# Routed experts on one core: tokens kept as a high and a low part, and one gather of 256 columns for every two rounds

## The chip, the core and the metric

The kernel runs on one core of a Trainium2 chip. A core has five engines with their own instruction streams: TensorE (PE: matmuls, with PEld its weight loads), VectorE (DVE), ScalarE (ACT), GpSimd (POOL, all but unused here) and SyncE (SP), which issues the DMA transfers from the chip's memory. They meet at semaphores. TensorE writes its results to eight PSUM banks of 128 x 512 floats, which ACT and DVE empty. The metric is the device time of one execution in microseconds (us).

## The reference

The reference is a whole two-block network over 256 tokens of width 1024. The part that matters is the last layer's mixture of experts. A router gives each token two of eight experts; expert e applies its own gated feed-forward net, and the token's result is the sum of its two experts' outputs, weighted by the router:

```python
h = rmsnorm(x, g)                      # 256 x 1024
top, idx = top_k(h @ router, 2); w = softmax(top)
for e in range(8):
    rows = tokens that chose e         # at most 128 in a round
    y[rows] += w * ((silu(h[rows] @ w_gate[e]) * (h[rows] @ w_up[e])) @ w_down[e])
x = x + gate * y                       # then a last rmsnorm
```

(The lines are a paraphrase. `w_gate` and `w_up` are 1024 x 3072, `w_down` 3072 x 1024, all float32.)

## The kernel before

All the rest of the network comes first and is not touched. `routed_feed_forward` computes the layer in **rounds**. A round takes one expert and up to 128 of its tokens. There is one round for each expert (0 to 7), and up to three more for experts with over 128 tokens; with these inputs there are 8 rounds. Round 0 is written out; rounds 1 to 7 are one loop on every engine, whose count is read from a table that the router's results fill.

**Weights.** A round reads 36 **tiles** of 1 MB: `n` = 0 to 23 are gate and up weights (for each of six `j`: two gate tiles, two up tiles), 24 to 35 are down weights. SP loads a tile into one of four `wide` buffers as soon as DVE has finished with the tile that lay there. Precision is kept by splitting each float32 operand into two parts of the type float32r, on which TensorE works faster: ACT copies the tile to `wide_high` (rounded, L3739), DVE subtracts that from the tile to get `wide_low` (L3864), each in one of three buffers, and TensorE does 12 matmuls of 512 columns a tile: high x high (L3588), high x low (L3589), low x high (L3592). ACT may fill a `wide_high` buffer when TensorE has used the tile three before.

**Tokens.** `h_tokens` (`ht`) holds all 256 tokens of the layer, in float32. At the start of a round the round's tokens are needed in the first 128 columns of an operand, `xg_high` and `xg_low` (`x_hi`, `x_lo`). A *gather* picks them: a matmul of `ht` with a matrix of zeros and ones, `pick` (256 tokens x 128 places), in float32: 16 matmuls of 128 columns, into banks 6 and 7. Then ACT copies the banks to `x_hi` (L3714) and DVE subtracts to get `x_lo` (L3816). The gather of round k + 1 stands in round k's down part, after its sixth tile (`q == 5`, so tile 29), and its copies stand behind tile 32 on ACT and DVE. The last round gathers too, for a round that does not come. DVE makes the `pick` of the next round at tile 8 (L3779), and TensorE transposes `pick` for the way back after tile 3 (`turn_pick`).

**Results.** After a round's last tile ACT scales and rounds the output to `y_high` (L3724), DVE makes `y_low` (L3810), and TensorE *scatters* them back to the 256 tokens: 16 matmuls of 256 float32r columns (L3619, L3620), into banks 1, 3, 6 and 7. This is done in the next round, after its tiles 0 and 1. DVE adds the banks to `x` (L3822). The banks 0 and 1 (gate) and 2 and 3 (up) are used in turn by the j's, 4 and 5 hold the output, and 6 and 7 the transposed hidden values (L3632).

What each engine does is an order written out by hand; no scheduler changes it. Within a round DVE does, for each `n`, `low_tile(n)` first, and behind it at n = 1 the two `y_low`, at n = 3 to 6 two additions to `x` each, and at n = 8 `pick`; ACT does at n = 1 the two `y_high`.

## Time and profile before

| | |
|---|---|
| time, median of 3 runs | 2598.43 us (2598.34 to 2603.25) |
| the profiled execution's own time | 2601.54 us |
| its span, first to last instruction | 2599.7 us |
| stretch of the expert rounds | 1721 to 2586 us |
| period of a round | 107.0 us |
| PE busy in the span | 2542.3 us (98%) |
| DVE, ACT busy | 1987.1 us (76%), 1428.3 us (55%) |
| moved by DMA | 627.19 MB, 241 GB/s over the span |

A round's period is the distance between the starts of the gathers in the chain that ended last. The profile is one execution, whose own time lies 3.1 us above the median of the three. Busy time of the PE rows counts a matmul from its start to its modelled end, and matmuls overlap; how fast they follow each other is read from their starts.

### The profile page before, as it was taken

How to read it: one execution, taken by the hardware profiler on the slowest of the kernel's cores; microseconds unless marked ns; L12 is line 12 of the kernel's file. 1: busy time of each engine (PE TensorE's matmuls, PEld its weight loads, DVE VectorE, ACT ScalarE, POOL GpSimd, SP SyncE). 2: the span in 40 equal slices, each digit the busy share in tenths (PEclk: the TensorE clock that was granted, in tenths of full speed). 3: DMA queues.
4: the chain of work that ended last, by engine and by line, in shares of the span. 5: the costliest groups of instructions: out<-in, count | busy, mean ns of one | idle time of the engine just before them, and what ended most of it. 6: DMA issues, size and time to landing. Idle time of an engine off the chain costs nothing. (4 is left out here: it accounts for less than half of the span.)

```text
span 2599.7 us, 41703 instructions
## 1 busy us (share of the span) xinstructions
PE 2542.3 (98%) x14574; PEld 2213.4 (85%) x14574; DVE 1987.1 (76%) x2776; ACT 1428.3 (55%) x1835; POOL 0.2 (0%) x4
## 2 busy tenths in 40 slices
PE   9999999998999999999999999999999999999998
PEld 5798889897888888888889999878888888888887
DVE  6688378896787777776856645569889889898897
ACT  4654243384544444444544434457777677777775
POOL 0000000000000000000000000000000000000000
PEclk8999899999999999999999999999999999999999
DMA  8423335425788878776434555359999999999995
GB/s 344 150 98 105 117 126 159 140 81 175 241 294 295 300 266 289 266 282 211 145 127 135 185 180 166 108 202 371 337 354 358 343 373 339 353 361 338 353 359 223
DMA packets 223747, 627.19 MB, mean 241 GB/s; under 512 B 15344, under 2 KB 23568, under 8 KB 223376
## 3 DMA queue, kind: packets, MB, share of 16 engines
q1 hardware_dynamic: 223632, 625.64, 68.6%
q8 instruction: 75, 1.23, 0.2%
q14 instruction: 40, 0.33, 0.0%
HBM read 619.29 MB, written 6.29 MB: 241 GB/s over the span
## 5 line engine op out<-in xcount | busy, mean ns | idle before, releaser
L3864 DVE TENSOR_TENSOR wide_low<-wide,wide_high 128x2048 fp32r<-128x2048 f32 x288 | 657.8, 2290 | 98.5 <-ACT wide_high L3739 96.4
L3739 ACT ACTIVATE wide_high<-wide 128x2048 fp32r<-128x2048 f32 x288 | 552.4, 1918 | 198.8 <-PE bank L3592 131.5
L232 DVE TENSOR_TENSOR expert_tile_low<-slot,expert_tile_high 128x1024 fp32r<-128x1024 f32 x216 | 263.6, 1223 | 119.2 <-ACT expert_tile_high L224 115.6
L224 ACT ACTIVATE expert_tile_high<-slot 128x1024 fp32r<-128x1024 f32 x216 | 227.4, 1054 | 182.1 <-PE bank L242 64.1
L3588 PE MATMUL bank<-wide_high,xg_high 128*128 128x512 f32 x768 | 303.8, 396 | 2.5 <-DVE xg_low L3816 2.5
L3589 PE MATMUL bank<-wide_high,xg_low 128*128 128x512 f32 x768 | 300.2, 391 | 0.0
L3592 PE MATMUL bank<-wide_low,xg_high 128*128 128x512 f32 x768 | 205.7, 390 | 0.0
L241 PE MATMUL bank<-h_high,expert_tile_high 128*128 128x256 f32 x704 | 173.4, 284 | 0.0
L2102 PE MATMUL bank<-expert_tile_high,act_hi 128*128 128x512 f32 x512 | 161.6, 397 | 11.9 <-DVE act_lo L2253 11.9
L242 PE MATMUL bank<-h_low,expert_tile_high 128*128 128x256 f32 x704 | 172.6, 283 | 0.0
L3588 PEld LDWEIGHTS bank<-wide_high,xg_high 128*128 128x128 f32 x768 | 144.8, 189 | 31.4 <-DVE xg_low L3816 2.7
L3592 PEld LDWEIGHTS bank<-wide_low,xg_high 128*128 128x128 f32 x768 | 144.1, 188 | 30.5 <-DVE wide_low L3864 0.2
L3589 PEld LDWEIGHTS bank<-wide_high,xg_low 128*128 128x128 f32 x768 | 144.9, 189 | 29.0
L2102 PE MATMUL bank<-expert_tile_high,act_lo 128*128 128x512 f32 x512 | 160.0, 394 | 0.0
L3588 PE MATMUL bank<-wide_high,moe_hid_high 128*128 128x512 f32 x384 | 151.7, 395 | 0.0
L3589 PE MATMUL bank<-wide_high,moe_hid_low 128*128 128x512 f32 x384 | 149.7, 390 | 0.0
L241 PEld LDWEIGHTS bank<-h_high,expert_tile_high 128*128 128x128 f32 x704 | 134.3, 191 | 13.0 <-issue 10.1
L232 DVE TENSOR_TENSOR layer_tile_low<-slot,layer_tile_high 128x1024 fp32r<-128x1024 f32 x66 | 80.9, 1226 | 80.0 <-ACT layer_tile_high L224 80.0
L2184 ACT ACTIVATE act_hi<-act_g 128x256 fp32r<-128x256 f32 x128 | 52.9, 413 | 159.4 <-DVE act_g L2248 158.8
L2108 PE MATMUL bank<-expert_tile_low,act_hi 128*128 128x512 f32 x512 | 138.2, 392 | 0.0
L242 PEld LDWEIGHTS bank<-h_low,expert_tile_high 128*128 128x128 f32 x704 | 134.7, 191 | 2.9
L224 ACT ACTIVATE layer_tile_high<-slot 128x1024 fp32r<-128x1024 f32 x66 | 70.1, 1062 | 112.5 <-PE bank L242 106.6
(611 smaller groups left out, 5129.8 us busy)
## 6 DMA issues: line engine op xcount, KB each, us to landing
wide<-in_moe_gu SPq DMA_DIRECT2D x192, 1024.0 KB, 6.0
wide<-in_moe_d SPq DMA_DIRECT2D x96, 1024.0 KB, 6.3
slot<-in_peer_u SPq DMA_DIRECT2D x128, 512.0 KB, 4.5
slot<-in_peer_v SPq DMA_DIRECT2D x128, 512.0 KB, 4.6
slot<-in_w_in SPq DMA_DIRECT2D x72, 512.0 KB, 3.6
picked_or_ada<-in_ada_w SPq DMA_DIRECT2D x48, 512.0 KB, 5.1
ada_slot<-in_ada_w SPq DMA_DIRECT2D x48, 512.0 KB, 4.7
slot<-in_ffn_gu SPq DMA_DIRECT2D x48, 512.0 KB, 3.6
```

The costliest lines, as they stand in the source:

```text
L224: core.nc.scalar.activation(self.tile_hi[:, place % 2], core.slot[u][:], ACT.Copy).then_inc(self.hi_ready.sem, 1)
L232: core.nc.vector.tensor_tensor(self.tile_lo[:, place % 2], slot[:], self.tile_hi[:, place % 2].bitcast(F32), ALU.subtract)\
L241: nc.tensor.matmul(out(c), self.tile_hi[:, place % 2, c, :], high(c), start=opens(c), stop=False, skip_group_check=not whole)
L242: last = nc.tensor.matmul(out(c), self.tile_hi[:, place % 2, c, :], low(c), start=False, stop=False, skip_group_check=not whole)
L2102: last = nc.tensor.matmul(core.bank[4 + 2 * tt + b][:, :], tokens(part, tt), v_hi[:, b, :], start=False, stop=False, skip_group_check=True)
L2108: last = nc.tensor.matmul(core.bank[4 + 2 * tt + b][:, :], tokens(act_hi, tt), v_lo[:, b, :], start=False, stop=stop, skip_group_check=True)
L2184: nc.scalar.activation(act_hi[:, w, :], act_g[:, w, :], ACT.Copy).then_inc(act_high.sem, 1)
L3588: nc.tensor.matmul(out(s), high(s), part(hi, s), start=s in opens, stop=False, skip_group_check=True)
L3589: nc.tensor.matmul(out(s), low(s), part(hi, s), start=False, stop=False, skip_group_check=True)
L3592: last = nc.tensor.matmul(out(s), high(s), part(lo, s), start=False, stop=s in closes, skip_group_check=True)
L3739: nc.scalar.activation(w_hi[n % NB][:].rearrange("p c n -> p (c n)"), wide[n % U][:], ACT.Copy).then_inc(hi_ready.sem, 1)
L3864: nc.vector.tensor_tensor(w_lo[n % NB][:].rearrange("p c n -> p (c n)"), wide[n % U][:], w_hi[n % NB][:].rearrange("p c n -> p (c n)").bit ...
```

## The change

The change touches `routed_feed_forward` alone.

- **Tokens as two parts.** `ht` is split once, in round 0: ACT copies it to `ht_hi` (behind its tile 8), DVE subtracts to get `ht_lo` (behind its tile 9), which takes the room of `ht`. From then on a gather is float32r: `ht_hi` with `pick` gives the high part in one bank, `ht_lo` with `pick` the low part in another. ACT and DVE each copy their own bank, and DVE no longer waits for ACT.
- **Rounds in pairs.** The rounds are now FIRST (0), then a loop of three over a pair EVEN and ODD (1 and 2, 3 and 4, 5 and 6; the names count within a pair), then a loop ALONE over the rest (7 and any more). `pick`, `x_hi` and `x_lo` hold two rounds side by side. DVE makes two `pick`s at n = 8 of FIRST and ODD, one in ALONE, none in EVEN.
- **Where the gathers are.** No round gathers at tile 29 any more. EVEN opens with `gather_two` (32 matmuls of 256 columns, in four groups of eight), and the scatter of the round before stands right behind it, before tile 0. ODD gathers nothing, and scatters after its tiles 0 and 1, as before. ALONE opens with `gather_alone` (32 matmuls of 128 columns), then the scatter. FIRST keeps the float32 gather.

```diff
+            def gather_two(i):
+                pe.wait_ge(picks.sem, picks.at(2) + i)
+                pe.wait_ge(hid_ready.sem, hid_ready.at(J) + i * (2 * J))
+                for g in range(4):
+                    if g == 3:
+                        pe.wait_ge(x_high.sem, x_high.at(1) + opened(EVEN, i))
+                        pe.wait_ge(x_ready.sem, x_ready.at(1) + opened(EVEN, i))
+                    for part, bank in ((ht_hi, GATHERED[g][0]), (ht_lo, GATHERED[g][1])):
+                        for j in range(2):
+                            c = 2 * g + j
+                            for tt in range(2):
+                                last = nc.tensor.matmul(core.bank[bank][:, 2 * M * j:2 * M * j + 2 * M], part[:, tt, c * P:c * P + P],
+                                                        pick[:, tt].rearrange("p r m -> p (r m)"), start=(tt == 0), stop=(tt == 1))
+                    last.then_inc(gathered.sem, 1)
+    GATHERED = ((6, 7), (1, 3), (0, 2), (6, 7))
+    GATHERED_ALONE = ((0, 6), (2, 7))
...
+            def scatter(k, kind, i):
                 pe.wait_ge(backs.sem, backs.at(1) + k)
-                pe.wait_ge(x_ready.sem, x_ready.at(2) + k * 2)
                 for s in range(4):
                     if s % 2 == 0:
                         pe.wait_ge(y_split.sem, y_split.at(s // 2 + 1) + k * 2)
+                    if kind == EVEN:
+                        pe.wait_ge(x_high.sem, x_high.at((2, 2, 4, 4)[s]) + opened(kind, i))
+                        pe.wait_ge(x_ready.sem, x_ready.at((2, 2, 4, 4)[s]) + opened(kind, i))
+                    if kind == ALONE and s >= 2:
+                        pe.wait_ge(x_ready.sem, x_ready.at(s - 1) + opened(kind, k))
...
+                if kind == EVEN:
+                    gather_two(i)
+                if kind == ALONE:
+                    gather_alone(k)
+                if kind in (EVEN, ALONE):
+                    scatter(k, kind, i)
...
-                    if q == 5:
-                        pe.wait_ge(hid_ready.sem, hid_ready.at(J) + k * J)
-                        gather(k + 1)
...
+            def copy_two(i):
+                for g in range(4):
+                    act.wait_ge(gathered.sem, gathered.at(g + 1) + opened(EVEN, i))
+                    nc.scalar.activation(x_hi[:, 2 * g:2 * g + 2, :, :], core.bank[GATHERED[g][0]][:, :].rearrange("p (c r m) -> p c r m", c=2, r=2), ACT.Copy)\
                         .then_inc(x_high.sem, 1)
...
+                    if n == C and kind == FIRST:
+                        nc.scalar.activation(ht_hi[:], ht[:], ACT.Copy).then_inc(tokens_high.sem, 1)
...
+            def low_two(i):
+                for g in range(4):
+                    dve.wait_ge(gathered.sem, gathered.at(g + 1) + opened(EVEN, i))
+                    nc.vector.tensor_copy(x_lo[:, 2 * g:2 * g + 2, :, :], core.bank[GATHERED[g][1]][:, :].rearrange("p (c r m) -> p c r m", c=2, r=2))\
+                        .then_inc(x_ready.sem, 1)
...
+                    if n == C + 1 and kind == FIRST:
+                        dve.wait_ge(tokens_high.sem, tokens_high.at(1))
+                        nc.vector.tensor_tensor(ht_lo[:], ht[:], ht_hi[:].bitcast(F32), ALU.subtract).then_inc(tokens_low.sem, 1)
```

`copy_two` stands behind `keep_outputs` (the two `y_high`) at ACT's n = 1, and `low_two` behind the two `y_low` at DVE's n = 1; before, both copies stood at n = 32.

On TensorE, in the down part of a round of the kernel before (L3588, L3589 and L3592 are a tile's three kinds of matmul, L3605 the gather), the program has:

```order
L3588 MATMUL bank<-wide_high,moe_hid_high 128x512
L3589 MATMUL bank<-wide_high,moe_hid_low 128x512
L3592 MATMUL bank<-wide_low,moe_hid_high 128x512 x4
L3605 MATMUL bank<-pick,h_tokens 128x128 x16
L3588 MATMUL bank<-wide_high,moe_hid_high 128x512
L3589 MATMUL bank<-wide_high,moe_hid_low 128x512
```

On TensorE, in the changed kernel, between the last tile of the round before and tile 0 of an EVEN round (L3640 is the new gather, L3671 and L3672 the scatter, L3611 a tile's last four matmuls), it has:

```order
L3611 MATMUL bank<-wide_low,moe_hid_high 128x512 x4
...
L3640 MATMUL bank<-pick,h_tokens_high 128x256 x4
L3640 MATMUL bank<-pick,h_tokens_low 128x256 x4
L3640 MATMUL bank<-pick,h_tokens_high 128x256 x4
L3640 MATMUL bank<-pick,h_tokens_low 128x256 x4
L3640 MATMUL bank<-pick,h_tokens_high 128x256 x4
L3640 MATMUL bank<-pick,h_tokens_low 128x256 x4
L3634 ISA
L3640 MATMUL bank<-pick,h_tokens_high 128x256 x4
L3640 MATMUL bank<-pick,h_tokens_low 128x256 x4
...
L3671 MATMUL bank<-back,y_high 128x256
```

The gather has left the middle of the down part and stands at the seam of two rounds, where its last group (behind the wait of L3634) uses banks 6 and 7 a second time.

On DVE, at tile 1 of an EVEN round of the changed kernel (L3955 is `wide_low`, L3889 `y_low`, L3907 the copies of the low parts), the program has:

```order
L3955 TENSOR_TENSOR wide_low<-wide,wide_high 128x2048
L3888 ISA
L3889 SCALAR_TENSOR_TENSOR y_low<-bank,shares_of_places,y_high 128x512
L3888 REGISTER_ALU
L3889 SCALAR_TENSOR_TENSOR y_low<-bank,shares_of_places,y_high 128x512
L3906 ISA
L3907 CAST xg_low<-bank 128x512
...
L3955 TENSOR_TENSOR wide_low<-wide,wide_high 128x2048
```

Four such copies now stand between `y_low` and the `wide_low` of tile 2, which before followed `y_low` at once.

On DVE, in round 0 of the changed kernel, from tile 8 on (L3858 is `pick`, L3964 the split of the tokens, L3986 the hidden values), the program has:

```order
L3858 TENSOR_SCALAR pick<-const,first,place_cols 128x128 x4
L3885 COPY shares_of_tokens<-shares 128x2
L3955 TENSOR_TENSOR wide_low<-wide,wide_high 128x2048
L3964 TENSOR_TENSOR h_tokens_low<-h_tokens,h_tokens_high 128x2048
L3986 TENSOR_TENSOR hid_r<-silu_r,bank 128x512
L3955 TENSOR_TENSOR wide_low<-wide,wide_high 128x2048
```

Two more `pick`s and the split of `ht` stand between the low parts of tiles 8 and 10.

## Rows read from the trace of the kernel before

**Rows 1.** The page, part 1: busy time and share of the span.

```profile
span 2599.7 us, 41703 instructions
PE 2542.3 (98%) x14574; PEld 2213.4 (85%) x14574; DVE 1987.1 (76%) x2776; ACT 1428.3 (55%) x1835; POOL 0.2 (0%) x4
```

**Rows 2.** Windows: one round, part of it, and a stretch around a gather.

```profile
core 0: us, PE busy (x) PEld busy (x) DVE busy (x) ACT busy (x) POOL busy (x), PEclk, DMA share, GB/s
1942.00:2049.00 107.00, 107.00 (x512) 89.51 (x510) 94.88 (x66) 77.23 (x53) 0.00 (x0) 1.00 0.98 353
1957.00:2020.00 63.00, 63.00 (x291) 52.11 (x290) 58.07 (x41) 46.35 (x32) 0.00 (x0) 1.00 0.99 353
1814.00:1819.00 5.00, 5.00 (x40) 4.72 (x39) 4.15 (x3) 3.07 (x4) 0.00 (x0) 1.00 1.01 392
```

**Rows 3.** Waits in the rounds (1721 to 2600): us in total, times, longest.

```profile
ACT wide_high L3739 <- PE bank L3592: 131.5, 151, 2.3
ACT wide_high L3739 <- DMA wide<-in_moe_gu: 37.2, 48, 3.1
ACT wide_high L3739 <- DMA wide<-in_moe_d: 29.2, 28, 1.8
PE bank L3588 <- DVE xg_low L3816: 2.5, 1, 2.5
PEld bank L3592 <- DVE wide_low L3864: 0.2, 1, 0.2
```

**Rows 4.** Chain that ended last, in order of time: start, us, what.

```profile
1815.11 3.57 PE bank L3605 x32
...
1922.23 3.57 PE bank L3605 x32
...
2564.43 3.57 PE bank L3605 x32
```

**Rows 5.** Timeline of PE around a scatter, 1840 to 1843: start, us, engine.

```profile
1840.29 0.28 PE L3619 MATMUL bank<-back,y_high 128*128 128x256 f32 x1
...
1842.08 0.28 PE L3620 MATMUL bank<-back,y_low 128*128 128x256 f32 x1
...
1842.20 0.40 PE L3588 MATMUL bank<-wide_high,xg_high 128*128 128x512 f32 x1
```

**Rows 6.** Groups by line and form, 1700 to 2600: busy, mean ns, idle before.

```profile
L3605 PE MATMUL bank<-pick,h_tokens 128*128 128x128 f32 x288 | 33.7, 275 | 0.8 <-DVE pick L3779 0.8
L3816 DVE TENSOR_TENSOR xg_low<-bank,xg_high 128x512 fp32r<-128x512 f32 x18 | 11.5, 682 | 0.0
L3714 ACT ACTIVATE xg_high<-bank 128x512 fp32r<-128x512 f32 x18 | 10.4, 589 | 6.9 <-PE bank L3605 6.8
L3880 DVE CAST back<-bank 128x256 fp32r<-128x256 f32 x8 | 3.3, 414 | 0.0
```

**Rows 7.** Timelines of PE, ACT and DVE where round 2 begins.

```profile
1941.06 1.07 PE L3592 MATMUL bank<-wide_low,moe_hid_high 128*128 128x512 f32 x4
1941.97 0.39 PE L3588 MATMUL bank<-wide_high,xg_high 128*128 128x512 f32 x1
1941.72 1.27 ACT L3724 ACTIVATE y_high<-bank,shares_of_places 128x512 fp32r<-128x512 f32 x2 [0.35 <-PE bank L3592]
1943.68 1.40 DVE L3810 SCALAR_TENSOR_TENSOR y_low<-bank,shares_of_places,y_high 128x512 fp32r<-128x512 f32 x2
1945.00 4.48 DVE L3864 TENSOR_TENSOR wide_low<-wide,wide_high 128x2048 fp32r<-128x2048 f32 x2
```

**Rows 8.** Timelines of round 0: ACT tiles 8, 9; DVE tiles 9, 10; PE tile 10.

```profile
1747.46 1.91 ACT L3739 ACTIVATE wide_high<-wide 128x2048 fp32r<-128x2048 f32 x1
1752.09 0.60 DVE L3779 TENSOR_SCALAR pick<-const,first,place_cols 128x128 f32<-128x128 f32 x2
1752.66 2.29 DVE L3864 TENSOR_TENSOR wide_low<-wide,wide_high 128x2048 fp32r<-128x2048 f32 x1
1754.87 0.68 DVE L3887 TENSOR_TENSOR hid_r<-silu_r,bank 128x512 f32<-128x512 f32 x1
1755.46 2.29 DVE L3864 TENSOR_TENSOR wide_low<-wide,wide_high 128x2048 fp32r<-128x2048 f32 x1
1759.94 1.07 PE L3592 MATMUL bank<-wide_low,xg_high 128*128 128x512 f32 x4
```

**Rows 9.** Timeline of DVE and PE where the weights came latest.

```profile
1890.05 2.29 DVE L3864 TENSOR_TENSOR wide_low<-wide,wide_high 128x2048 fp32r<-128x2048 f32 x1 [2.39 <-ACT wide_high L3739]
1892.43 0.93 PE L3592 MATMUL bank<-wide_low,xg_high 128*128 128x512 f32 x3
```

More of the change, by code:

```diff
@@ L3537, in routed_feed_forward, with opened @@
         "outputs_low", "outputs_scattered", "outputs_added", "share_columns", "picks_turned"))
+    tokens_high, tokens_low = core.count("tokens_high"), core.count("tokens_low")
+    PAIRED = (EXPERTS - 2) // 2
+    FIRST, EVEN, ODD, ALONE = range(4)
+    ALONE_FROM = 2 * PAIRED + 1
+    def opened(kind, i):
+        return 0 if kind == FIRST else i * 4 + 2 if kind == EVEN else i * 2 + (2 + 4 * PAIRED - 2 * ALONE_FROM)
+    place_of = lambda kind: 1 if kind == ODD else 0
     J = D_FF // 512
@@ L3566, in _ @@
             sp.wait_ge(table_made.sem, table_made.at(1))
-            with sp.Fori(1, n_rounds(sp)) as k:
+            with sp.Fori(0, PAIRED) as i:
+                for r in range(1, 3):
+                    load(i * 2 + r, i * 2 + r, 0)
+            with sp.Fori(ALONE_FROM, n_rounds(sp)) as k:
                 load(k, expert_of(sp, k), 0)
@@ L3686, in round_ @@
                     else:
-                        turn_pick(k)
+                        turn_pick(k, place)
                 for q in range(T2):
@@ L3694, in round_ @@
                         turn(k, J - 1)
-                    if q == 5:
-                        pe.wait_ge(hid_ready.sem, hid_ready.at(J) + k * J)
-                        gather(k + 1)
             pe.sem_inc(scattered.sem, 4)
-            round_(0)
+            round_(0, FIRST, 0)
             pe.wait_ge(table_made.sem, table_made.at(1))
-            with pe.Fori(1, n_rounds(pe)) as k:
-                round_(k)
-            scatter(n_rounds(pe))
+            with pe.Fori(0, PAIRED) as i:
+                round_(i * 2 + 1, EVEN, i)
+                round_(i * 2 + 2, ODD, i)
+            with pe.Fori(ALONE_FROM, n_rounds(pe)) as k:
+                round_(k, ALONE, None)
+            scatter(n_rounds(pe), FIRST, None)
             for c in range(C):
@@ L3753, in round_ @@
                             .then_inc(hid_high.sem, 1)
-                    if n == 1 and not isinstance(k, int):
+                    if n == 1 and kind != FIRST:
                         keep_outputs(k)
-                    if n == 32:
-                        copy_gathered(k + 1)
+                        if kind == EVEN:
+                            copy_two(i)
+                        if kind == ALONE:
+                            copy_gathered(kind, k)
             act.sem_inc(y_kept.sem, 2)
             high_tile(0, 0)
-            copy_gathered(0)
-            round_(0)
+            copy_gathered(FIRST, 0)
+            round_(0, FIRST, 0)
             act.wait_ge(table_made.sem, table_made.at(1))
-            with act.Fori(1, n_rounds(act)) as k:
-                round_(k)
+            with act.Fori(0, PAIRED) as i:
+                round_(i * 2 + 1, EVEN, i)
+                round_(i * 2 + 2, ODD, i)
+            with act.Fori(ALONE_FROM, n_rounds(act)) as k:
+                round_(k, ALONE, None)
             keep_outputs(n_rounds(act))
@@ L3774, in _, with make_picks @@
         def _(dve):
-            def make_pick(k):
-                e = k if isinstance(k, int) else expert_of(dve, k)
-                for tt in range(2):
-                    ins = nc.vector.tensor_scalar(pick[:, tt, :], core.iota, first[:, bass.ds(k, 1)], place_cols[:, tt, bass.ds(e, 1)],
-                                                  ALU.add, ALU.is_equal)
+            def make_picks(k, n=1):
+                for r in range(n):
+                    e = k + r if isinstance(k, int) else expert_of(dve, k + r)
+                    for tt in range(2):
+                        ins = nc.vector.tensor_scalar(pick[:, tt, r, :], core.iota, first[:, bass.ds(k + r, 1)], place_cols[:, tt, bass.ds(e, 1)],
+                                                      ALU.add, ALU.is_equal)
                 ins.then_inc(picks.sem, 1)
@@ L3900, in _ @@
             take_shares(0)
-            low_gathered(0)
-            round_(0)
-            with dve.Fori(1, n_rounds(dve)) as k:
-                round_(k)
+            low_gathered_first()
+            round_(0, FIRST, 0)
+            with dve.Fori(0, PAIRED) as i:
+                round_(i * 2 + 1, EVEN, i)
+                round_(i * 2 + 2, ODD, i)
+            with dve.Fori(ALONE_FROM, n_rounds(dve)) as k:
+                round_(k, ALONE, None)
             rounds = n_rounds(dve)
```

104 lines of the change are left out of this document (67 added, 37 removed).

## Prediction

> **What bounds the kernel now.** I read the page first: TensorE is busy 98% of the span [rows 1]. Then the windows of one round: TensorE 107.00 of 107.00 us at a granted clock of 1.00, which is the level of 2.4 GHz, DVE 94.88, ACT 77.23, and the DMA share 0.98 [rows 2]. The table of waits says who waits: ACT waits 131.5 us for TensorE to use tiles, TensorE 2.5 us once for the first `xg_low`, and 0.2 us for a tile [rows 3]. So the rounds last as long as TensorE's instructions do, and an instruction taken from it is time won, unless DVE or the DMA, both near their limit, then come too late.
>
> **What is removed.** The chain shows each gather inside a round as one piece of 3.57 us [rows 4]; there are eight, of rounds 0 to 7, and the last serves no round. That is 8 x 3.57 = 28.6 us. The copies behind them (two of 589 ns on ACT, two of 682 ns on DVE [rows 6]) were hidden behind matmuls and give nothing by themselves.
>
> **What an EVEN round's opening costs.** The new gather has 32 float32r matmuls of 256 columns, each with its own weights. The scatter has the same form: 16 matmuls between 1840.29 and 1842.20 [rows 5], so 0.119 us each. A group of eight is 0.96 us, all of it 3.82 us. But the operands are needed at once. Let 0 be the seam, 1941.97 in the row of L3588. ACT has finished `y_high` at 1942.99, at 1.0. DVE is in `wide_low` of tile 1, then `y_low`, and is free at 1945.00, at 3.0 [rows 7]. From there:
> TensorE does groups 0 to 2 from 0 to 2.9, and must then wait: group 3 takes banks 6 and 7 again, so ACT and DVE must both have emptied them. ACT did so at about 1.8. DVE begins at 3.0; a copy of 512 columns costs 0.68, since 256 take 414 ns and the old subtraction of 512 took 682 [rows 6]. So group 3 runs from 3.75 to 4.7, after a wait of about 0.9. The first two parts of the scatter use banks 1 and 3, empty by then: 4.7 to 5.65. The last two need DVE's fourth copy, which begins when group 3 has drained, at 4.9, and ends at 5.6: no wait. They end at 6.6, and tile 0 starts. Of this the scatter's 1.9 us was paid before too, two tiles later. An opening adds 4.7 us, three add 14.1. The bounds: 3.8 each if DVE is early (11.5 in all), 6.5 each if every group waits for its copies (19.5).
>
> Queued behind the copies on DVE is `wide_low` of tile 2, and behind that SP's load of tile 6. ACT is free at 5.6, so it has split tile 2 at 7.5, and DVE at 9.8. TensorE does four matmuls in 0.91 us, 1941.06 to 1941.97 [rows 7], so a tile in 2.73, and comes to the low part of tile 2 at 6.6 + 2 x 2.73 + 1.8 = 13.9. That stall is hidden by 4 us. DVE has less in hand at tiles 6 to 11, where the additions to `x` and the hidden values stand between the tiles; I count it about 1 us ahead at tile 7, and cost it at nothing. If that cover went, it would be about 1 us a pair.
>
> **What the ALONE round's opening costs.** Its 32 matmuls have 128 columns, and no row shows float32r that narrow; each such matmul in the program has 256 or 512 columns. The lower end is the float32 gather's rate per instruction: x288 are 9 gathers of 32, and 3.57 / 32 is 0.112 us [rows 4, 6], which gives 3.6 us. The upper end is its rate per matmul (two instructions each), 0.223 us: 7.1 us. I take 7.0, from the only rows with the same 128 columns, the same weights and the same `pick`. The waits for `y_low` and the copies fall within it, and the scatter behind it is only moved. A rule of the Trainium skill speaks for the lower end: TensorE: Matmul & The Clock Gate, section "LDWEIGHTS", puts a load of 128 columns of weights at P / 1.2, 107 ns, and knows no surcharge for narrow float32r. By it the gather would take 3.4 us; no row here decides it.
>
> **What round 0 pays.** ACT splits `ht` behind tile 8: the form is a tile's, 1.91 us from about 1749.4 [rows 8], and tile 9 is high at 1753.1 and not 1751.7. DVE does four `pick`s where it did two (+0.5), `wide_low` of tile 9 until 1755.5, `ht_lo` as long as a tile's subtraction (2.2 net) to 1757.7, the hidden value to 1758.3, and then tile 10, ready at 1760.6. TensorE wants it at 1759.94 [rows 8]: it waits 0.6 us, and about nothing at tile 11. Bounds 0 and 3. Later ODD rounds make four `pick`s too, but have no split.
>
> **What the DMA costs.** The gather's pause let the weights catch up. Without it a round is 103.5 us, and 36 tiles must land every 2.87 us instead of 2.97, in the down part every 2.73. The windows show 353 GB/s at a share of 0.98 in a round, but 392 GB/s around a gather [rows 2], which is a tile in 2.68 us, so the engines can do more than they are asked. At the worst place `wide_low` was ready at 1892.34 and TensorE took it at 1892.43 [rows 9]. Such a dip now has no gather to heal it; I add 0.5 us, bounds 0 and 8. The Trainium skill speaks against the change here: HBM Reference, section "Specifications (TRN2)", gives a core 358 GB/s as its share. At that rate 36 tiles take 105.4 us, so each of the four rounds that no opening lengthens would lose 1.9 us, 7.7 in all. The window of 392 GB/s says that this is no cap for us; the page itself says that a core streaming alone gets about 425.
>
> **The sum.** -28.6 + 14.1 + 7.0 + 0.6 + 0.5 = -6.4 us. The profiled execution took 2601.5, so it would take 2595.1. It lay 3.1 above the median of 2598.4; the same difference from the median gives 2592.0 us, or 0.25% less. What measurement of this kernel can tell from no change is about 0.2%, 5.2 us: 2593.2.
>
> **Rivals.**
> *Narrow matmuls run at full pace.* ALONE's gather then costs 3.8 (32 x 0.119), and the time is 2588.8. For it: 256 columns take 0.119 us and 512 take 0.228 (0.91 / 4), so the time goes by the width [rows 5, 7]. Against it: no row is that narrow.
> *The openings or the loads cost more.* The copies run in step with the groups (+5.4 us at the upper bound), or a few tiles come late after a seam without a pause (+1 to +6). For it: the DVE is the busiest engine next to TensorE, and ACT already waits 37.2 + 29.2 us for tiles [rows 3]. Against it: TensorE waited for a tile 0.2 us in 860. The time is 2594 to 2598, about 2596.
> *Slower: the transfers take over.* If 353 GB/s is what they can give (a share of 0.98 to 0.99 [rows 2] reads so), 36 tiles take 107 us whatever TensorE does. Then the 28.6 us are not won, but for the last gather's 3.6; and as SP may load only when DVE has split, which the copies delay, a part of the openings is added. With half of them, (14.1 + 7.0) / 2 + 0.6 - 3.6 = +7.6: 2606. It decides once tiles land slower than one in 2.87 us over a whole round. Against it are the 392 GB/s, and that ACT waits twice as long for TensorE as for tiles [rows 3].
>
> **How the numbers follow.** As computed, within 1.5 us: 0.50. Narrow at full pace: 0.20. Openings or loads dearer: 0.20. Slower: 0.08. Something that wins more than all of this: 0.02. The likeliest is 2592.0 us. The first case is faster by over 0.2% in about three quarters (0.38), the second is, the last is: 0.60. Same: 0.12 of the first, and 0.19 of the third: 0.31. Slower: 0.09. The range of 2588.0 to 2597.5 takes in the first two, nearly all of the third, and leaves out some 0.12.
>
> **What would show it.** The gather's matmuls of 256 columns follow each other at 0.12 us, with one idle time of about 0.9 us in each of three openings, ended by DVE's copy of the low part; 6.6 us from the seam to tile 0. ALONE's gather takes 7 us (a pace of 0.22) or under 4 (0.12). One wait of about 0.6 us for `wide_low` of tile 10 in round 0. The pair of rounds has a period of about 212 us (2 x 103.5 + 4.7) where it was 214. The prediction is wrong if 256 columns of `pick` are slower than 256 of `back`, if TensorE waits for tiles in the rounds' down parts, or if the narrow gather costs other than its bounds.

## The result and the profile after

The changed kernel is slower: 2612.08 us, the median of 5 runs (2606.08 to 2622.31), against 2598.43 us (2596.04 to 2603.25, 5 runs) for the kernel before beside it. The ratio is 1.0060 with a 95% interval of 1.0044 to 1.0075. The forecast was 2592.0 us, faster. The profiled execution, at 2606.08 us, is the fastest of the five; a second trace of this kernel comes with the experiments.

The page, busy time and share, answers to [rows 1]:

```profile
span 2604.3 us, 41430 instructions
PE 2536.0 (97%) x14446; PEld 2204.8 (85%) x14446; DVE 1988.0 (76%) x2777; ACT 1428.6 (55%) x1834; POOL 0.2 (0%) x4
```

TensorE is busy 6.3 us less than before, and yet the span is 4.6 us longer: idle time came. The windows (us, busy of each engine, granted clock, DMA share, GB/s) of one stretch as long as in [rows 2], and of the openings of rounds 1, 3 and 5, show where:

```profile
1942.00:2049.00 107.00, 103.95 (x481) 86.56 (x480) 92.84 (x64) 74.95 (x51) 0.00 (x0) 0.98 0.96 350
1822.00:1840.00 18.00, 14.67 (x81) 13.23 (x80) 12.96 (x10) 8.85 (x9) 0.00 (x0) 0.91 0.84 286
2041.00:2057.00 16.00, 12.67 (x66) 11.28 (x65) 9.84 (x9) 9.16 (x9) 0.00 (x0) 0.79 0.86 315
2259.00:2278.00 19.00, 13.37 (x66) 12.07 (x65) 10.19 (x9) 9.18 (x9) 0.00 (x0) 0.73 0.69 255
```

In the three stretches around these openings TensorE is idle 3.3 to 5.6 us each, and the granted clock, 1.00 in every window of [rows 2], is 0.91, 0.79 and 0.73. The table of waits over the rounds (us in total, times, longest), beside [rows 3]:

```profile
ACT wide_high L3810 <- DMA wide<-in_moe_gu: 79.4, 88, 4.1
ACT wide_high L3810 <- PE bank L3611: 71.4, 85, 3.2
ACT wide_high L3810 <- DMA wide<-in_moe_d: 52.2, 59, 2.7
PE bank L3640 <- issue: 9.0, 4, 4.5
PE bank L3640 <- DVE xg_low L3907: 3.3, 1, 3.3
PE bank L3671 <- DVE y_low L3889: 1.4, 2, 1.1
PE bank L3607 <- ACT xg_high L3779: 1.0, 1, 1.0
PE bank L3611 <- DVE wide_low L3955: 0.6, 2, 0.4
```

Three readings. ACT waits twice as long for tiles as before (131.6 against 66.4 us), but TensorE waits for a tile only 0.6 us: the transfers became tight and did not take over. TensorE waits once for the low copies, for 3.3 us, where three waits of 0.9 were forecast. And it waits 9.0 us for "issue", that is for nothing which the profile records; there is no such wait inside the rounds before. The name alone proves little: at the first tile of round 0 a wait of 2.5 us is put down to `xg_low` in the trace of before, and one of 2.6 us to "issue" in seven of the other traces, three of them without a loop of pairs.

To compare kernels whose first 1,720 us differ a little from run to run, I split the expert stage of each trace. A tile is marked by the start of its last four matmuls (low x high); two tiles without anything between them are 2.72 us apart. The **opening** of a round is the distance from tile 35 to tile 0 less 2.72; a round's **inside** runs from tile 0 to tile 35. For round 3 of the changed kernel the timeline gives both marks, and an opening of 2056.84 - 2041.85 - 2.72 = 12.27 us:

```profile
2041.85 1.07 PE L3611 MATMUL bank<-wide_low,moe_hid_high 128*128 128x512 f32 x4
2056.84 1.07 PE L3611 MATMUL bank<-wide_low,xg_high 128*128 128x512 f32 x4
```

| kernel (profiled run) | openings of rounds 1 to 7 | openings, sum | insides, sum | stage |
|---|---|---|---|---|
| before | 0 in all | 0 | 832.7 | 851.7 |
| changed | 10.8, 0, 12.3, 0.1, 15.3, 0, 6.4 | 44.9 | 797.8 | 861.8 |

(The stage runs from tile 0 of round 0 to tile 35 of round 7: openings, insides and seven times 2.72 us.) The insides gave back 34.9 us. That is the eight gathers (28.6) and four scatters that moved into openings (4 x 1.96 = 7.8), less 1.5 us of new waits. The openings took 44.9 us for it, of which 7.8 are the moved scatters. The stage is 10.1 us longer and the span only 4.6, since round 0's first tile came 5.6 us earlier in this execution.

**How an opening is lost.** Timelines of TensorE, ACT and DVE at the opening of round 1, which no jump back precedes (start, us, engine, line):

```profile
1827.02 0.64 PE L3640 MATMUL bank<-pick,h_tokens_high 128*128 128x256 f32 x4
1829.38 0.64 PE L3640 MATMUL bank<-pick,h_tokens_low 128*128 128x256 f32 x4
1833.35 0.96 PE L3640 MATMUL bank<-pick,h_tokens_high 128*128 128x256 f32 x4 [3.33 <-DVE xg_low L3907]
1834.11 1.05 PE L3640 MATMUL bank<-pick,h_tokens_low 128*128 128x256 f32 x4
1826.97 1.92 ACT L3810 ACTIVATE wide_high<-wide 128x2048 fp32r<-128x2048 f32 x1 [1.74 <-DMA wide<-in_moe_gu]
1828.79 1.25 ACT L3795 ACTIVATE y_high<-bank,shares_of_places 128x512 fp32r<-128x512 f32 x2
1828.99 2.29 DVE L3955 TENSOR_TENSOR wide_low<-wide,wide_high 128x2048 fp32r<-128x2048 f32 x1 [1.37 <-ACT wide_high L3810]
1831.20 1.40 DVE L3889 SCALAR_TENSOR_TENSOR y_low<-bank,shares_of_places,y_high 128x512 fp32r<-128x512 f32 x2
1832.52 1.88 DVE L3907 CAST xg_low<-bank 128x512 fp32r<-128x512 f32 x3
```

Read it from the bottom. DVE's first copy of gathered tokens starts at 1832.52, because `y_low` and, ahead of it, the split of tile 1 come first in its order. DVE began to split tile 1 at 1828.99, because ACT had waited 1.74 us for that tile to land. The seam was at 1827.02, so `y_low` starts 4.2 us behind it; at the seam of [rows 7] it was 1.7. TensorE has done three groups by 1830.0 and stands still for 3.33 us. What follows is slow as well: four matmuls take 0.85 us (1834.96 - 1834.11) where the same four took 0.47 before the pause.

At the opening of round 3 a jump back of the loop comes first. Timelines of TensorE and DVE:

```profile
2045.96 1.22 PE L3640 MATMUL bank<-pick,h_tokens_high 128*128 128x256 f32 x4 [3.05 <-issue]
2046.98 1.05 PE L3640 MATMUL bank<-pick,h_tokens_low 128*128 128x256 f32 x4
2050.66 0.58 PE L3640 MATMUL bank<-pick,h_tokens_high 128*128 128x256 f32 x1 [0.28 <-issue]
2052.94 0.28 PE L3671 MATMUL bank<-back,y_high 128*128 128x256 f32 x1
2047.03 2.29 DVE L3955 TENSOR_TENSOR wide_low<-wide,wide_high 128x2048 fp32r<-128x2048 f32 x1 [1.46 <-ACT wide_high L3810]
2049.24 1.40 DVE L3889 SCALAR_TENSOR_TENSOR y_low<-bank,shares_of_places,y_high 128x512 fp32r<-128x512 f32 x2
```

TensorE does nothing for 3.05 us, waiting for no other engine by the profile, and then works at half pace. No wait for `xg_low` is left at this opening: DVE's copies are done before TensorE comes to them. Windows of short stretches show its granted clock, ahead of the pause in round 1 and behind the pauses of rounds 1, 3 and 5:

```profile
1826.00:1827.00 1.00, 1.00 (x6) 0.82 (x5) 1.00 (x1) 0.03 (x1) 0.00 (x0) 1.00 1.02 389
1833.00:1836.00 3.00, 2.65 (x13) 2.68 (x14) 2.09 (x4) 0.80 (x2) 0.00 (x0) 0.60 0.99 316
2046.00:2051.00 5.00, 4.72 (x20) 4.42 (x21) 3.97 (x4) 3.27 (x5) 0.00 (x0) 0.50 1.07 383
2265.00:2274.00 9.00, 7.71 (x34) 7.42 (x35) 4.88 (x7) 2.14 (x5) 0.00 (x0) 0.50 0.75 276
```

0.50 is the level of 1.2 GHz. The queues of the DMA engines have the other half of the story: packets that carry instructions. First before, from 1715 to 1942 (round 0 and the first pass of its loop); from 1942 to 2585 the view of that kernel shows no instruction packet at all:

```profile
q8 instruction: 9, 0.15, 0.2%
q14 instruction: 7, 0.06, 0.1%
```

And the changed kernel, from 1942 to 2585:

```profile
q8 instruction: 29, 0.48, 0.3%
q14 instruction: 16, 0.13, 0.0%
```

(Packets, MB, share.) A loop body of one round is fetched once; one of two rounds is fetched again in every pass: of the 29 packets on q8, 10 move between 2042 and 2258 us and 11 between 2260 and 2480, which are the second and the third pass. One of them moves right behind each jump back, from 2043.3 to 2044.3 us (TensorE starts again at 2045.96) and from 2262.4 to 2263.5 (it starts at 2265.19).

### The profile page after: what moved, and what is told of

Its sections match the earlier page's. It is cut to its first block and busy times, and to the rows that moved or that the text cites. A ratio compares the mean times of both kernels' runs of the same rounds, so it can differ in the third digit from the quotient of the medians.

```text
span 2604.3 us, 41430 instructions
## 1 busy us (share of the span) xinstructions
PE 2536.0 (97%) x14446; PEld 2204.8 (85%) x14446; DVE 1988.0 (76%) x2777; ACT 1428.6 (55%) x1834; POOL 0.2 (0%) x4
## 5 line engine op out<-in xcount | busy, mean ns | idle before, releaser
L3955 DVE TENSOR_TENSOR wide_low<-wide,wide_high 128x2048 fp32r<-128x2048 f32 x288 | 656.6, 2288 | 102.1 <-ACT wide_high L3810 97.2
L3611 PE MATMUL bank<-wide_low,xg_high 128*128 128x512 f32 x768 | 206.2, 390 | 0.6 <-DVE wide_low L3955 0.6
L3611 PEld LDWEIGHTS bank<-wide_low,xg_high 128*128 128x128 f32 x768 | 143.5, 188 | 32.5 <-DVE wide_low L3955 2.5
L241 PEld LDWEIGHTS bank<-h_high,expert_tile_high 128*128 128x128 f32 x704 | 134.9, 192 | 13.1 <-issue 10.1
```

The source lines that it names most:

```text
L241: nc.tensor.matmul(out(c), self.tile_hi[:, place % 2, c, :], high(c), start=opens(c), stop=False, skip_group_check=not whole)
L3611: last = nc.tensor.matmul(out(s), high(s), part(lo, s), start=False, stop=s in closes, skip_group_check=True)
L3955: nc.vector.tensor_tensor(w_lo[n % NB][:].rearrange("p c n -> p (c n)"), wide[n % U][:], w_hi[n % NB][:].rearrange("p c n -> p (c n)").bit ...
```

## The experiments

The theory after this reading had three parts: **A**, TensorE stalls at a jump back of a long body, since its instructions have to be fetched again; **D**, the copies stand behind a tile 1 that lands late (the first four expectations call it B, seams); and the half clock, which follows from either pause. The rivals: the transfers of the weights (**C**), and the gather's own cost. (Some later expectations give B and C another meaning and say which.) Each run's table row gives the median, the ratio to the kernel before in the same job with its 95% interval, and the split of its trace.

| run | median us | ratio | openings of 1, 3, 5, 7 | others | insides | stage |
|---|---|---|---|---|---|---|
| two-round bodies | 2600.36 | 1.0007 (0.9998 to 1.0016) | 0, 1.1, 1.2, 0 | 0 | 832.7 | 854.0 |
| changed, written out | 2604.09 | 1.0023 (1.0012 to 1.0034) | 7.7, 10.8, 12.0, 7.1 | 0 | 797.2 | 853.8 |
| gather at tile 29, loops | 2598.73 | 1.0001 (0.9987 to 1.0015) | 0, 2.9, 4.3, 5.5 | 0 | 818.7 | 850.4 |
| gather at 29, written out | 2587.51 | 0.9954 (0.9942 to 0.9966) | 0, 0, 0, 8.3 | 0.1 | 816.7 | 844.2 |
| before, written out | 2598.22 | 0.9993 (0.9984 to 1.0001) | 0, 0, 0, 0 | 0 | 832.6 | 851.6 |
| copies first, written out | 2591.61 | 0.9971 (0.9962 to 0.9980) | 5.9, 7.6, 6.7, 5.5 | 0 | 796.8 | 841.5 |
| no gather in the loop | 2580.36 | 0.9924 (0.9910 to 0.9938) | 0, 0.2, 0, 0 | 0 | 813.4 | 832.6 |
| at 29, copies first in 7 | 2586.75 | 0.9951 (0.9938 to 0.9964) | 0, 0, 0, 5.5 | 0 | 814.4 | 838.9 |
| copies first, loops | 2611.71 | 1.0038 (1.0024 to 1.0051) | 6.1, 13.4, 14.7, 5.5 | 0.2 | 805.5 | 864.6 |
| changed again | 2612.87 | 1.0047 (1.0033 to 1.0061) | 11.7, 13.0, 13.7, 7.1 | 0 | 801.4 | 865.8 |
| jump at a plain seam | 2595.41 | 0.9981 (0.9970 to 0.9992) | 5.9, 6.5, 6.0, 5.5 | 3.9 (round 4) | 803.0 | 849.9 |

### Bodies of two rounds in the kernel before

```diff
-            with pe.Fori(1, n_rounds(pe)) as k:
+            with pe.Fori(0, 3) as i:
+                round_(i * 2 + 1)
+                round_(i * 2 + 2)
+            with pe.Fori(7, n_rounds(pe)) as k:
                 round_(k)
```

The same on ACT and DVE. 

> The kernel before, with its gathers where they were; only the loops of TensorE, ScalarE and VectorE have a body of two rounds (three times), and one more loop for round 7 and on. No instruction is added to a round. Theory A (code: a body of two rounds does not stay with the engine and is fetched again on every pass, so that TensorE waits at each jump back and then runs at the lower clock for a while): 5 to 15 us slower than before, idle time of TensorE ended by 'issue' at two seams, instruction transfers through all rounds. Rival B (seams: the loss is in waits for the copies and in late tiles at the openings): no change, within 2 us. Rival C (the weights come too late when the gather's pause is gone): no change.

Theory A's 5 to 15 us missed. The trace shows 1.13 and 1.16 us of opening at the two seams with a jump back to the two-round body, and nothing elsewhere; the time does not tell it from no change. The instruction packets from 1715 to 2610 are 37 and 12 on the two queues, where the kernel before has 9 and 7. So a long body is fetched again without the new gather too, and costs little by itself.

### The changed kernel with its pairs written out

```diff
-            with pe.Fori(0, PAIRED) as i:
+            for i in range(PAIRED):
                 round_(i * 2 + 1, EVEN, i)
                 round_(i * 2 + 2, ODD, i)
```

> The changed kernel with rounds 1 to 6 written out one behind the other instead of a loop of three pairs. Theory A: the waits called 'issue' at the second and third opening (3.3 and 5.6 us in the trace of the changed kernel) and the half pace behind them go, so 8 to 14 us less than the changed kernel, about 2600. Rival B: the openings stay as long as they are, 2612. Rival C: no change, 2612.

It wins back about 8 us (2604.1 against 2612, of two jobs; by the ratios 6 to 10), the lower end of what theory A said, and no "issue" wait ahead of the gather's matmuls is left. But the openings still take 7.7 to 12.0 us, with 8.4 us of waits for `xg_low` in three. The two openings at the jumps fell by 4.8 us together (12.3 and 15.3 to 10.8 and 12.0; 3.9 against the second trace). Part A is real, and it is not all.

### The pair's gather back at tile 29, in loops and written out

The 256-column gather is kept, and moved from the opening of EVEN to the down part of the round ahead: groups 0 to 2 behind tile 29, group 3 behind tile 31, the copies behind tiles 32 and 34, the scatter behind tile 1 again. ALONE stays as changed.

```diff
-                if kind == EVEN:
-                    gather_two(i)
...
+                    if q in (5, 7) and kind in (FIRST, ODD):
+                        gather_two(0 if kind == FIRST else i + 1, (0, 1, 2) if q == 5 else (3,))
```

In loops (the last pass gathers once for nothing): 

> The changed kernel with its loop of pairs, but the gather of two rounds stands in the down part of the round before (three groups behind tile 29, the fourth behind tile 31, copies behind tiles 32 and 34), and all scatters of the pairs stand behind tile 1. The last pair gathers once more than is needed (3.8 us). Without any code wait it would be 28.6 less, 4 x 3.8 + 4.6 + 0.7 more than before: 2590. Theory A: the waits at two jumps back stay, 5 to 12 us: 2595 to 2602. Rival B (seams): 2590. Rival C (late tiles): over 2600, with waits of TensorE for wide_low all through the rounds.

Written out (without that gather): 

> Both: rounds 1 to 6 written out, and the gather of two rounds in the down part of the round before; no superfluous one but the opening of round 7 as in the changed kernel. Theory A: -28.6 + 3 x 3.8 + 4.6 + 0.7 = 12 us less than before, 2586 to 2588. Rival B: the same. Rival C (late tiles): 2595 or more, with waits for tiles.

Both times are where theory A put them. In loops it only comes back to the time of before; written out it beats it by 0.46%. The openings of rounds 3 and 5, at the jumps back, account for 7.2 us between the two; TensorE has an "issue" wait of 2.6 us at each. (The medians differ by 11.2 us, the stages by 6.2; the superfluous gather takes 3.9 of it.) The gather of two rounds at once costs 3.88 us inside a round (104.61 against 100.73), where two float32 gathers cost 7.14.

### The kernel before, written out

```diff
-            with pe.Fori(1, n_rounds(pe)) as k:
+            for k in range(1, 7):
+                round_(k)
+            with pe.Fori(7, n_rounds(pe)) as k:
                 round_(k)
```

> The kernel before with rounds 1 to 6 written out one behind another in place of the loop's passes; nothing else changes. The run with the pair gather at tile 29, written out, took 0.9954 of the kernel before, against 1.0001 for the same order in loops. If writing out is worth something only where the body of a pass is long (theory A: code that the jump back fetches again stalls TensorE, and the kernel before, with a body of one round, shows no such stall), this kernel takes as long as before: 2599.7, within 2 us. If writing out gives TensorE something in any kernel (rival B), it falls by some of the 12 us by which the two runs at tile 29 differ: 2588 to 2595. If the program's longer code costs fetches as it runs (rival C), it is slower by 2 to 5 us: 2602 to 2605.

No change that can be measured, and each of the seven openings stays at 0. It too has instruction packets from 1942 to 2585 (24 and 10, against 29 and 16 in the changed kernel), and TensorE never waits for them. This straight code is fetched in time, and the body of one round needs no second fetching. Writing out gains only where a long body jumps back.

### Copies ahead of tile 1, written out

```diff
-                    if n == 1 and kind != FIRST:
+                    if n == (1 if kind == ODD else 0) and kind != FIRST:
                         keep_outputs(k)
```

The same on DVE with `low_outputs`; the rest is the changed kernel written out. 

> The changed kernel, written out, with one edit: the copies of the gathered tokens and of the last outputs stand ahead of the split of tile 1 on ScalarE and VectorE instead of behind it, in the openings that gather. In the written-out run the openings of rounds 1, 3, 5 and 7 took 7.7, 10.8, 12.0 and 7.1 us more than a seam without gathering, and the copies stood behind a tile 1 that had landed late. Theory D (the copies' place behind a late tile 1 makes most of it): each of the openings of rounds 1, 3 and 5 comes down to 5 to 7 us, 15 us in all less for the three, and the kernel takes about 2590. Rival E (late tiles stay late, the wait just moves to tile 1's own matmuls): openings as before, 2603 to 2605, with waits of TensorE for tile 1's parts in place of those for the copies. Rival F (the wait is the gather's own, the copy after the last matmul): 2 to 3 us less, 2601.

The time fell by 12.5 us (again between two jobs; the ratios went from 1.0023 to 0.9971), the openings by 12.0 (37.6 to 25.6). The three that gather two rounds now average 6.7 us, one of them, at 7.6, above the 5 to 7 expected, and the clock in the windows of all three is 1.00. The window of round 3's opening, and timelines of TensorE and DVE there, to be held against those of the changed kernel:

```profile
2038.00:2050.00 12.00, 10.56 (x69) 9.49 (x68) 9.00 (x9) 8.61 (x10) 0.00 (x0) 1.00 0.79 290
2038.92 0.64 PE L3643 MATMUL bank<-pick,h_tokens_high 128*128 128x256 f32 x4
2043.37 0.71 PE L3643 MATMUL bank<-pick,h_tokens_high 128*128 128x256 f32 x4 [1.44 <-DVE xg_low L3910]
2043.92 0.63 PE L3643 MATMUL bank<-pick,h_tokens_low 128*128 128x256 f32 x4
2039.01 2.29 DVE L3958 TENSOR_TENSOR wide_low<-wide,wide_high 128x2048 fp32r<-128x2048 f32 x1 [1.40 <-ACT wide_high L3813]
2041.22 1.40 DVE L3892 SCALAR_TENSOR_TENSOR y_low<-bank,shares_of_places,y_high 128x512 fp32r<-128x512 f32 x2
2042.54 1.87 DVE L3910 CAST xg_low<-bank 128x512 fp32r<-128x512 f32 x3
```

Tile 0's split (2039.01) is followed by `y_low` and the copies at once; one wait of 1.44 us is left, and the matmuls behind it keep their pace. Tile 1 is split late in exchange, at 2047.09, and TensorE does not wait for it. Theory D holds.

### No gather in the loop

```diff
-                    if q == 5:
+                    if q == 5 and first_round:
                         pe.wait_ge(hid_ready.sem, hid_ready.at(J) + k * J)
                         gather(k + 1)
```

> The kernel before, leaving out the gathering of rounds 2 to 7: their matmuls and the copies behind them are gone, and those rounds multiply the tokens of round 1 again, so that what is computed is not the reference's. It prices all that any change to the gather can give. The gather is 3.57 us a round and is made in seven of them (in rounds 1 to 7 of the loop, the last for nothing). Theory (the gather is TensorE's time and nothing else binds): 7 x 3.57 = 25.0 us less, 2574.7. Rival C (the weights' transfers are the bound as soon as TensorE spends less in a round): the round stays near 101 us where it was 104.4, with waits of TensorE for tiles' parts inside the rounds: 2580 to 2590, and the rounds' transfers at a rate no higher than in the kernel before.

It won 19.4 us of the 25.0 and stands at the fast end of rival C's range. Rounds 4 to 7 gave their full 3.6 us, rounds 1 and 3 3.3 and 3.4; in round 2 late tiles took back 4.8 us (105.54 against 100.73), and round 0 lost 0.6. Windows of about a round each, from round 4 on:

```profile
2145.00:2249.00 104.00, 104.00 (x482) 86.41 (x482) 94.36 (x64) 76.38 (x51) 0.00 (x0) 1.00 1.00 365
2249.00:2352.00 103.00, 103.00 (x478) 85.60 (x477) 93.45 (x64) 75.79 (x50) 0.00 (x0) 1.00 0.99 365
2352.00:2456.00 104.00, 104.00 (x482) 86.45 (x481) 94.26 (x64) 76.62 (x51) 0.00 (x0) 1.00 1.00 365
```

Rival C is thereby limited, not refuted: the transfers can keep up with rounds 3.57 us shorter (36 tiles in 103.45 us, 365 GB/s) for rounds on end, and in one round they did not.

### The best order, with copies first in round 7

The written-out gather at tile 29, with `n == (0 if kind == ALONE else 1)` for the copies. 

> The run with the pair gather at tile 29, written out, which took 2587.5, with the copies of round 7's opening alone put ahead of the split of tile 1. That opening cost 8.3 us beyond a plain seam in its trace; with theory D it comes down to about 5.5, so 2584.5 to 2586.5. With its rival (the wait moves to tile 1) the time stays at 2587.5.

The opening of round 7 fell as expected, from 8.3 to 5.5 us. Not all of the 2.8 us is the wait itself: at 8.3 TensorE had stood for 1.03 us, and its granted clock was 0.50 from 2472 to 2474 us behind that. The time, 0.8 us lower, misses its range by 0.3 and does not tell the two kernels apart. Both beat the kernel before by 12 to 13 us.

### Copies first in the loops, and the changed kernel again

The one edit of the copies, with the loops kept. 

> The changed kernel as it is, in its loops, with the one edit of the run before it: copies of the last outputs and of the gathered tokens ahead of the split of tile 1 in the openings that gather. Written out, this edit took 12 us off (2604.1 to 2591.6). If the place of the copies and the refetching of code at the jumps back add up independently, 8 to 13 us come off here as well, to 2597 to 2602 where the changed kernel takes 2610, and TensorE still waits for nothing that the profile shows at the openings of rounds 3 and 5, 3 to 4.5 us each. If the refetching hid behind the wait for the copies (rival), less comes off, 4 to 7 us: 2603 to 2606. If the idle stretch was what dropped the clock in two openings and the copies made it so long, the clock stays at full in all openings and 13 to 16 us come off: 2595 to 2597.

The changed kernel once more, in the same job. 

> The changed kernel itself, once more, beside the run above on the same chip, since its five times spread over 16 us. By its trace it takes 10 us more than the kernel before in the expert stage: 2608 to 2614, a ratio of 1.004 to 1.006.

All three expectations for the loops missed: 1.2 us less than the changed kernel, where its repetition came out as before. The trace says why. Round 1's opening, behind no jump, fell from 11.7 to 6.1; those of rounds 3 and 5 did not fall at all. TensorE at round 3's opening:

```profile
2047.73 1.06 PE L3640 MATMUL bank<-pick,h_tokens_high 128*128 128x256 f32 x4 [4.48 <-issue]
2048.59 1.05 PE L3640 MATMUL bank<-pick,h_tokens_low 128*128 128x256 f32 x4
2051.15 0.60 PE L3640 MATMUL bank<-pick,h_tokens_high 128*128 128x256 f32 x3
2052.64 0.39 PE L3640 MATMUL bank<-pick,h_tokens_high 128*128 128x256 f32 x1 [0.89 <-issue]
2053.81 0.64 PE L3640 MATMUL bank<-pick,h_tokens_low 128*128 128x256 f32 x4
```

The two stalls make 5.4 us, and the 16 matmuls up to 2051.15, at 0.213 instead of 0.119 us, another 1.5. Taken off the 13.4 us they leave 6.5, within the 5.9 to 7.6 that an opening costs written out. The refetching and the late copies overlap: while TensorE stands at the jump, DVE gets its work done anyway. At those two openings together the copies' edit alone gave nothing (28.1 us, against 27.6 and 26.7 in the two traces of the changed kernel), writing out alone 3.9 to 4.8, and both together 12.4 to 13.3. The rest of the missing gain is inside the rounds (805.5 against 797.8 and 801.4 us), where tiles came late.

### The jump back at a plain seam

```diff
-            with pe.Fori(0, PAIRED) as i:
-                round_(i * 2 + 1, EVEN, i)
+            round_(1, EVEN, 0)
+            with pe.Fori(0, PAIRED - 1) as i:
                 round_(i * 2 + 2, ODD, i)
+                round_(i * 2 + 3, EVEN, i + 1)
+            round_(2 * PAIRED, ODD, PAIRED - 1)
```

> The run with loops and the copies ahead of tile 1, with the passes cut at another place: round 1 stands ahead of the loop, a pass is a round without gathering and then one with it (2 and 3, then 4 and 5), and round 6 stands behind the loop. The body is as long as before, but the jump back now comes at a plain seam, with the tokens of the round ready in SBUF, and the openings that gather are reached inside a pass. In the run before, TensorE waited 5.4 and 6.4 us for nothing that the profile shows in the openings behind the jumps, and ran some 20 matmuls at half pace. If the wait belongs to the jump back and is only as long as it is because the instructions behind it are many and short (gather and scatter, 0.119 us each), it shrinks to the 1.1 us that the kernel before with bodies of two rounds paid at a plain seam, and the openings come down to the 6 to 7.5 us of the written-out run: 2592 to 2597. If the wait belongs to the length of the body whatever follows the jump (rival), 5 us stay at the one jump back that is left: 2597 to 2602. If it belongs to the opening itself, not to the jump, nothing changes: 2610 to 2612.

2595.4 us, within the first range, and 16 less than the run before with a body as long, which it jumps back to once and not twice. The openings that gather are at 5.9, 6.5 and 6.0, as written out, and the one jump back costs 3.9 us at the seam of round 4, more than the 1.1 expected and less than the rival's 5. TensorE there waits 2.09 us for nothing recorded (timeline), and the window behind it has the low clock, which makes the rest:

```profile
2151.31 0.79 PE L3610 MATMUL bank<-wide_high,xg_high 128*128 128x512 f32 x1 [2.09 <-issue]
```

```profile
2151.00:2155.00 4.00, 3.69 (x9) 2.98 (x10) 4.00 (x5) 1.86 (x1) 0.00 (x0) 0.57 0.67 217
```

So the wait belongs to the jump back, and it is longer where the gather follows the jump than at a plain seam. The packets' times in the traces say more. At each jump back, us from the seam (the end of the round's last matmuls, as above) to the start of the last q8 packet ahead of TensorE's next matmul, from the seam to that matmul, and the difference:

| jumps back | packet | TensorE | between |
|---|---|---|---|
| kernel before, two-round bodies | -1.8, -1.7 | 1.0, 1.0 | 2.8, 2.7 |
| gather at tile 29, loops | -0.1, -0.1 | 2.8, 2.8 | 2.9, 2.8 |
| jump at a plain seam | -0.5 | 2.3 | 2.7 |
| changed kernel, both traces | 0.6, 1.9, 1.3, 1.6 | 3.2, 4.7, 4.2, 4.4 | 2.7, 2.8, 2.9, 2.8 |
| copies first, loops | 1.9, 2.5 | 4.8, 5.3 | 2.9, 2.8 |

From the start of the packet to TensorE's next matmul it is 2.7 to 2.9 us in all eleven. What differs is how early the packet starts: ahead of the seam in the bodies that begin with tiles, behind it in those that begin with the gather. (In three of the eleven another q8 packet starts 2.2 to 2.5 us earlier.) Why it starts when it does is not shown.

## Why the prediction was wrong

**What is removed**: right. Rounds that neither gather nor scatter run 98.77 us inside, those that only scatter 100.73, and before it was 104.31. 104.31 - 100.73 is 3.58 for a gather, against 3.57.

**An EVEN round's opening**: this step failed. It was put at 4.7 us plus the moved scatter's 1.9, 6.6 from seam to tile 0, and took 10.8, 12.3 and 15.3. Less the moved scatter that is 32.5 us where 14.1 were counted, 18.4 more, and this alone turns the sum from -6.4 to +12. In the three openings TensorE stood still for 12.3 us (3.3, 3.3 and 5.6) where 2.7 were counted, and most of the other 8.8 us is matmuls at half the clock, which the prediction had at nothing. Two premises under it were wrong. (1) "DVE ... is free at 1945.00, at 3.0" was read off a seam that had a gather's pause 16 us ahead of it, and carried over to seams that have none. In the changed kernel DVE's `y_low` starts 4.2 to 6.5 us after the seam at the three openings. With the copies put ahead of tile 1, and no jump, the openings come to 5.9, 7.6 and 6.7 us, an average of 6.7: the working was sound for an order that the change does not have. (2) The loop body was taken to cost nothing. No rival spoke of the program's own instructions; the refetching behind the jumps comes with 3.3 us of idle TensorE at round 3's opening and 5.6 at round 5's (the four "issue" waits are 9.0 in all), and the half clock behind each pause adds to it. The rival that had the time rise did so by transfers that take over, and that is not what happened: the rounds' insides kept their gain.

The loss is not the sum of the two. Removing the refetching alone gave 8 us, moving the copies alone about 1, which these runs can't tell from nothing, both together some 20 (2612 to 2591.6).

**The ALONE round's opening**: right in mechanism, too dear in size. The narrow gather runs from 2480.73, 32 matmuls in 3.6 us:

```profile
2480.73 1.00 PE L3653 MATMUL bank<-pick,h_tokens_high 128*128 128x128 f32 x8
2483.36 1.06 PE L3653 MATMUL bank<-pick,h_tokens_low 128*128 128x128 f32 x8
2484.71 0.39 PE L3671 MATMUL bank<-back,y_high 128*128 128x256 f32 x1 [0.29 <-DVE y_low L3889]
```

That is 0.112 us a matmul, the lower end of the two. The rule of the Trainium skill that spoke for it, TensorE: Matmul & The Clock Gate, section "LDWEIGHTS", with 107 ns for a load of 128 columns, comes within 5 ns of the 112 measured. I had taken the other end since its rows looked nearer; they were of float32, which takes two instructions a matmul, and that was the difference that counted. With waits the opening costs 4.5 us beyond the moved scatter, not 7.0.

**Round 0**: 1.3 us more than its old length less the gather (100.12 against 102.38 - 3.57 = 98.81), forecast 0.6. In the six traces with this round 0 it is 0.7 to 2.1.

**The DMA**: 0.5 us was right to some tenths in the profiled run (the insides of rounds 1 to 7 are 0.4 us above 98.77 and 100.73), and it was some 3 us in its repetition (insides of 801.4). The share that the Trainium skill gives a core when both of a pair stream, 358 GB/s (HBM Reference, section "Specifications (TRN2)"), is not a cap here: without the gathers 365 to 369 GB/s went on for four rounds. But the transfers were not harmless. The prediction priced a late tile only by TensorE's wait for the tile itself; TensorE did wait for what stood behind the tile in ACT's and DVE's order.

In all: -28.6 + 32.5 + 4.5 + 1.5 = +9.9, and the traces' stages differ by 10.1 (0.1 is at the seam of round 4). The medians differ by 13.6 in both jobs, and the second trace of the changed kernel has a stage 4.0 us longer.

Why tile 1 is late at these seams is argued, not shown. At the seams behind a round with a gather (before, and the gather at tile 29) DVE begins tile 1 within 1.5 us of its usual time, and in the changed kernel, behind a round without one, up to 4.8 us later. Yet in the run without any gather in the loop it was late at only two seams. The rate that an EVEN round asks (36 tiles in 98.77 + 2.72 us, 372 GB/s) may be what drains the buffers for the round after it; no run sets it apart, and it can't be all, since DVE began tile 1 some 2.4 us late at the seam of round 1 too, with no EVEN round ahead of it.

## What to carry to other kernels

Work moved to a seam needs its consumers' engines at that moment: read what stands ahead of the copies in their order, and how late that can become, and not when the engine was free before. A body that grows from one round to two may no longer be held and be fetched again in each pass; look for instruction packets in the DMA view and for "issue" waits behind the jump, and put the jump at a plain seam, or write the rounds out. When two causes overlap at a place, undo them together too, since one alone may show little or nothing.

## What the runs showed of the hardware

- A loop body of one round (some 500 matmuls on TensorE) is fetched once, one of two rounds again in each pass: no instruction packets against 29 + 16 from 1942 to 2585. TensorE's next matmul comes 2.7 to 2.9 us after the start of the last q8 packet ahead of it, in eleven jumps back of six traces. The jump back then cost 1.1 to 1.2 us in the kernel before with two-round bodies, 2.9 to 4.3 at plain seams with the new gather's code in the body, and 3.3 to 6.4 of standing alone where the gather's short matmuls follow it.
- After each of the ten pauses of TensorE of 3 us or more in the openings the granted clock was 0.50 to 0.62 over the next 4 us, with 256-column matmuls at 0.213 us instead of 0.119 at the lower level. Of shorter pauses the length alone does not tell: after 2.61 us it stayed at 1.00 and after 2.60 it was 0.57 (both in the loops with the gather at tile 29); after 2.09 it was 0.57 (jump at a plain seam); after 1.44 and 1.57 it stayed at 1.00, and after 1.03 it was 0.57 (written out with the gather at tile 29, round 7).
- A float32r matmul of 128 columns with its own weights takes 0.112 us, half of float32's 0.223, and 256 columns take 0.119: the gather of two rounds costs hardly more than that of one (3.88 against 3.57 us inside a round).
